# The GLA decay's logarithms closed one norm step after the first sum, and the five turns given an item each

## What is computed

```
q  = partial_rope(rms_norm(q, q_g));  k = partial_rope(rms_norm(k, k_g))
qi = partial_rope(qi);                ki = partial_rope(rms_norm(ki, kidx_g))
log_a = log_sigmoid(ga @ gla_wa2 + gla_ba) / 16
b = cumsum(log_a) in each chunk;  GLA uses q*exp(b), k*exp(b_last - b), exp(b_last), ...
```

## Time and profile before

| what | us |
|---|---|
| median of three runs | 1944.82 |
| lowest and highest of them | 1942.38, 2065.7 |
| the profiled execution | 1947.0 |
| its span in the profile | 1945.2 |
| mean granted TensorE clock | 0.987 |
| PE, PEld busy in the span | 1854.0, 1780.1 |
| DVE, ACT, POOL busy | 770.6, 632.5, 700.7 |

### The profile page before, as it was taken

One profiled execution on the slowest core, in us unless ns is written; L12 is line 12 of the kernel. 1 busy time (PEld: TensorE's weight loads), 2 busy tenths in 40 slices (PEclk: granted clock), 3 DMA queues, 4 the chain that ended last, 5 costly groups with the idle time before them and its releaser, 6 DMA issues.

```text
span 1945.2 us, 33977 instructions
## 1 busy us (share of the span) xinstructions
PE 1854.0 (95%) x13982; PEld 1780.1 (92%) x13982; DVE 770.6 (40%) x1534; ACT 632.5 (33%) x1079; POOL 700.7 (36%) x376
## 2 busy tenths in 40 slices
PE   7988999999999999999999899989999999999999
PEld 6977888899999999999999778878899999999998
DVE  4645775235322212212425558642353221222232
ACT  4333214555432222212333322236543321222122
POOL 2313442433333434434333233425133334344342
PEclk8989999999999999999999999999999999999999
DMA  5222125211222232222223222241022222322222
GB/s 145 76 70 57 51 73 138 60 44 55 88 76 85 82 87 79 85 85 76 79 77 76 55 71 65 70 131 55 23 77 87 76 83 82 86 78 85 82 74 90
DMA packets 285700, 151.47 MB, mean 78 GB/s; under 512 B 17830, under 2 KB 284138, under 8 KB 285546
## 3 DMA queue, kind: packets, MB, share of 16 engines
q1 hardware_dynamic: 285546, 149.30, 27.3%
HBM read 141.89 MB, written 7.37 MB: 77 GB/s over the span
## 4 chain that ended last, share of the span: by engine, by line
PE 78%; DVE 11%; issue 3%; ACT 3%; SPq 2%; POOL 2%; DMA 1%; DVEq 0%; ACTq 0%; POOLq 0%
PE prod L1119 68%; PE aux L1488 2%; DVE scores L2293 1%; POOL w_lo L1520 1%; DVE top L2291 1%; PE aux L1189 1%; PE aux L1478 1%; SPq L959 1%; DVE in_lo L1939 1%; SPq L965 1%; PE aux L1250 1%; PE aux L1452 1%; DMA x_rows<-in_x_sample 1%; DVE qiz L2237 1%; PE aux L1134 1%
## 5 line engine op out<-in xcount | busy, mean ns | idle before, releaser
L1520 POOL TENSOR_TENSOR w_lo<-w_raw,w_hi 128x1024 fp32r<-128x1024 f32 (+1 forms) x246 | 598.6, 2433 | 1147.5 <-ACT w_hi L1613 1140.0
L1119 PE MATMUL prod<-in_hi,w_hi 128*128 128x288 f32 x2912 | 650.0, 305 | 12.8 <-DVE in_lo L2080 5.0
L1119 PE MATMUL prod<-in_lo,w_hi 128*128 128x288 f32 x2912 | 627.3, 297 | 0.0
L1119 PE MATMUL prod<-in_hi,w_lo 128*128 128x288 f32 x2912 | 627.2, 297 | 0.0
L1119 PEld LDWEIGHTS prod<-in_hi,w_hi 128*128 128x128 f32 x2912 | 470.0, 191 | 30.6 <-issue 18.8
L1119 PEld LDWEIGHTS prod<-in_lo,w_hi 128*128 128x128 f32 x2912 | 472.7, 190 | 0.0
L1119 PEld LDWEIGHTS prod<-in_hi,w_lo 128*128 128x128 f32 x2912 | 472.7, 190 | 0.0
L1613 ACT ACTIVATE w_hi<-w_raw 128x1024 fp32r<-128x1024 f32 (+1 forms) x246 | 254.8, 1036 | 273.7 <-PE prod L1119 273.7
L1119 PE MATMUL prod<-mid_hi,w_hi 128*128 128x288 f32 x960 | 207.7, 298 | 3.5 <-POOL w_lo L1520 3.4
L1119 PE MATMUL prod<-mid_hi,w_lo 128*128 128x288 f32 x960 | 206.4, 296 | 0.0
L1119 PE MATMUL prod<-mid_lo,w_hi 128*128 128x288 f32 x960 | 206.3, 296 | 0.0
(11 more groups left out here) (276 smaller groups left out, 1598.0 us busy)
## 6 DMA issues: line engine op xcount, KB each, us to landing
w_raw<-in_w_ffn_gu SPq DMA_DIRECT2D x88, 512.0 KB, 3.8
w_raw<-in_w_in SPq DMA_DIRECT2D x76, 512.0 KB, 3.8
w_raw<-in_w_ffn_down SPq DMA_DIRECT2D x32, 512.0 KB, 3.9
w_raw<-in_w_o SPq DMA_DIRECT2D x16, 512.0 KB, 4.0
w_raw<-in_w_ffn_down SPq DMA_DIRECT2D x16, 384.0 KB, 3.4
k_pages<-in_cache_k SPq DMA_DIRECT2D x32, 128.0 KB, 2.1
v_pages<-in_cache_v SPq DMA_DIRECT2D x32, 128.0 KB, 2.0
w_raw<-in_w_ob SPq DMA_DIRECT2D x16, 256.0 KB, 2.9
```

What stands on the lines that cost most here:

```text
L1119: ins = e.matmul(slot(g)[:, h, :], w[:, slot_w, i * P:(i + 1) * P], a[:, i, h * HALF:(h + 1) * HALF], start=first, stop=last)
L1520: e.tensor_tensor(w_lo[:, p % 2, 0:n], w_raw[:, p % RAW_RING, 0:n], w_hi[:, p % 2, 0:n].bitcast(F32), ALU.subtract).then_inc(w_lo_done, 1)
```

## The change

The list of items of this stage is written anew. The steps are the same in number and kind. The first tile's norm step goes ahead of `z` within one item; `z_min` goes from its place with `decay` to the head of the second tile's item; `decay` gets an item alone, and `decay_ref` goes with the fourth tile's norm, ahead of it; the five `qkT` stand at the end, one per item, with `decay_exp` and `qn_end` where they stood beside the second and third. There are 12 items instead of 11.

```
-        items = [[], [("z",)] + normed[0], normed[1], normed[2], [("z_min",), ("decay",)], normed[3],
-                 [("decay_ref",), ("qkT", 0)], normed[4] + [("qkT", 1), ("decay_exp",)], [("qn_end",), ("qkT", 2)],
-                 [("qkT", 3)], [("qkT", 4)]]
+        items = [[], normed[0] + [("z",)], [("z_min",)] + normed[1], normed[2], [("decay",)], [("decay_ref",)] + normed[3],
+                 normed[4], [("qkT", 0)], [("qkT", 1), ("decay_exp",)], [("qn_end",), ("qkT", 2)], [("qkT", 3)],
+                 [("qkT", 4)]]
         self.woven(range(first["gq"], first["gv"]), items)
```

## The result

The changed kernel takes 1922.86 us (median of four runs, 1922.6 to 1923.65), the kernel before beside it 1943.6 us. The ratio is 0.99 with a 95% interval of 0.9881 to 0.9919, a gain of 15.7 to 23.1 us. One of the four executions of before took 2065.7 us; the other three have the median 1942.38, which makes the gain 19.5 us instead of 20.7. The forecast was 1928.9 us and a gain of 15.9. The time lies inside the range (1922 to 1939), 0.9 us above its low end, and nearer to rival B's 1925.1 than to the forecast. A second measurement of the same kernel gave 1923.59 us against 1945.11, ratio 0.9889 (0.9872 to 0.9907).

What follows compares the result with a forecast made beforehand. It took TensorE, 78% of the chain, as the bound. Waits gave 9.5 us (13.3 less 3.8 new) and the clock 6.4, together 15.9: 1944.8 - 15.9 = 1928.9 us, range 1922 to 1939 for eight in ten.

Steps and rivals of the forecast that it cites:

- rival B: Second turn does not wait, through faster DVE references or ACT's queue giving way: gain 13.3 + 6.4, 1925.1 us; chance 0.12.
- The forecast case: Whole stage: old waits go, new second-turn waits come, clock recovers; gain 15.9 us, 1928.9 us; chance 0.46.
- the prediction's own sign: Second turn's wait for ACT's eviction L1758: 1 to 3 us expected; the step is wrong if missing or over 4 us.
- step (d): Second turn: TensorE newly waits 1.1 and 2.7 us for ACT's eviction; the four wait entries shrink by 9.5 us net.
- (a): ACT squares the first tile ahead of the logarithms; its 1.11 us hide in ACT's 2.56 us idle time, price nothing.
- (b): DVE closes the logarithms early, 2.9 and 1.3 us before TensorE's decay sums; both waits go, -9.3 us.
- (c): DVE's decay references, 5.7 us from 121.0 and 1078.7, finish in time; the first turn's waits go, -3.3 us.
- (e): TensorE's decay sums and the products behind them run at full clock: 2.6 + 1.8 + 2.0, together 6.4 us gained.
- A: TensorE's waits shrink but the clock stays low, or a new 2.7 us wait lowers it: gain 9.5, 1935.3 us; chance 0.22.
- C: DVE meets POOL's gk1 split; second turn waits up to 2.4 us more per layer: 1933.7 us; chance 0.15.
- D: TensorE starves for gk1's weights, copied behind a late root on ACT; slower, 1955 us; chance 0.03.
- E: The edit does nothing, since another releaser ends TensorE's decay wait: 1944.8 us; chance 0.02.

## Why the prediction was right, and where it was not

The time fell inside the range, but not on the path that was forecast. The forecast case, with a new wait at the second turn, did not come, and by the prediction's own sign step (d) was wrong. What came was rival B, to which it gave 0.12, and the range reached this time because B had pulled its low end to 1922. That the early closing takes the long waits and the low clock behind them away was forecast rightly, and so was the end of the first turn's waits. The forecast had 3.8 us of new waits that did not come.

(a) *The square first.* It cost nothing, as said: ACT squared in the gap, at 106.06, and the last logarithms began 4.50 us behind the first logits matmul, as with the square behind them. But I took the place for one without a price in either direction ("still hidden by (b)"). The run with the logarithms first shows 2.6 us per layer. I had the price of the square on ACT, and left out the chain from it through DVE's sum to the closing behind it.

(b) *The early closing.* Right. The closing was done at 113.42, both waits are gone, and the early closing by itself gives 15.4 of the stage's 22.2 us. I had 2.9 and 1.3 us of slack; it is 1.75 in both layers.

(c) *The references.* This is the step that failed. "DVE still meets POOL there, so it is free at 121.0" carried the 2.04 us multiplication over from the earlier trace rows. Yet the third tile's norm stands ahead of part 8 now, one part earlier, and thereby ahead of the copy for gk0 on ACT. DVE is done before POOL begins. From the end of the closing to the first reference it takes 116.95 - 113.42 = 3.5 us; in the run with the norm behind the copy 118.66 - 113.32 = 5.3. The parts' numbers were in the text of the change, and the copy's place between parts 8 and 9 could have been read from the order on ACT. I compared DVE's row without looking at what on the other engine decides it.

(d) *The second turn.* No wait came in after, so the net of 9.5 us for waits became the full 13.3. The mechanism was right under (c)'s premise: where the meeting was put back, the second turn waited for L1758 as forecast, 1.53 us in each layer against 1.1 and 2.7. In after that eviction ends at 127.09, 0.28 us before the turn needs its bank. So it is a narrow escape, and the runs with the logarithms first and with six delays both show the wait come back.

(e) *The clock.* Right in size. Decay sums with the restart: 4.80 - 2.37 = 2.4 us in layer 0 and 4.24 - 2.37 = 1.9 in layer 1, products 5.18 - 3.29 = 1.9, together 6.2 us against 6.4. The held-up closings show 1.7 to 2.4 us per layer from the other side. That fits layer 1; the 4.3 us of layer 0 are more, and why is not shown. The low stretch of layer 0 that I had left in was missing from the first trace of after and present in the second: chance, worth 1.5 us.

Waits 13.3 and clock 6.2 make 19.5 of the 22.2 us of the stage. The rest is the low stretch in layer 0, 1.5 us, and 1.2 us that were not split further. TensorE was not idle in them, since its idle time in the stage is the 13.3 us; restarts behind waits belong there (the run with the norm behind the copy lost 1.72 us for a wait of 1.53).

*The rivals.* B happened. DVE is through the references early, though not faster: they took 5.8 us (116.95 to 122.76) against the 5.7 forecast, and began earlier. A fell. Its premise, that a wait of 2.7 us brings the low clock back, holds in this stage (2.68 us did), but no such wait came. C did not happen in after. D did not: the split for gk1 ends at 126.68 + 2.37 = 129.05 and TensorE starts that panel behind the third turn, which begins at 131.29. E fell.

## What to carry to other kernels

Where two engines block each other, a row's duration belongs to its place in time: before carrying a 2.04 us row over, find out which copy or split decides the meeting, and whether the edit moves the step past it. A wait of TensorE is worth more than its length when the clock falls behind it, so remove the one long wait first, then check that the new order's slacks (1.75 and 0.28 us here) are as large as you think. When squares, sums and closings form a chain over two engines that a third waits for, price the order by the last link, not by the first.

## What the runs showed of the hardware that was not expected

- Of TensorE's waits in this stage, those from 0.92 to 1.66 us (at L1211, L1226) left the clock at 1.00, and those of 1.92, 2.57, 2.68, 3.93, 4.75 and 5.42 us came with half clock, 1.2 GHz. (The 1.14 and the 1.92 each had a low stretch of their own shortly ahead.) I had thought of 2.7 us as doubtful. (The Trainium skill, TensorE: Matmul & The Clock Gate, part on the clock gate, has the half clock return after idling; the longer waits agree.)
- What the half clock costs behind such a wait was 1.7 to 2.4 us, for waits from 2.57 to 4.75 us, and 4.3 us in layer 0 of the kernel before.
- Low-clock stretches come and go between two executions of the same program with no wait ahead of them: behind the logits in layer 0 in the repeat of after, not in the first trace. Of the 22 layers in the eleven traces, four have such a stretch (layer 0 of before, of the repeat of after and of the run with six delays, layer 1 of the run with all but the closing). Each began 2.6 to 3.7 us behind the first logits matmul; why there is not shown. In before such a stretch was paid for by the wait behind it, in after it costs 1.5 us.
